# The gate products of a block-diagonal recurrence: four 64x64 tiles in place of a 128x128 weight with zero blocks

## The reference, cut to what matters

```python
xc = depthwise_conv(x, conv_w, conv_b, (LRU_CONV_WIDTH - 1, 0))      # 4 taps
xb = xc.reshape(xc.shape[:-1] + (LRU_BLOCKS, LRU_BLOCK))             # 8 blocks of 64
r = sigmoid(einsum("blhi,hij->blhj", xb, w_r).reshape(xc.shape) + b_r)
i = sigmoid(einsum("blhi,hij->blhj", xb, w_i).reshape(xc.shape) + b_i)
log_a = -LRU_C * r * softplus(-lam)
a = exp(log_a)
bx = sqrt(-expm1(2.0 * log_a)) * (i * xc)
# h[t] = a[t] * h[t-1] + bx[t], forward (d = 0) and backward (d = 1), context first
```

## Time and profile before

| | us |
|---|---|
| median of three runs | 1327.19 (1326.09 to 1328.32) |
| profiled execution, span from first to last instruction | 1326.2 |
| TensorE matmul busy | 1263.8 |
| VectorE busy | 730.9 |
| ScalarE busy | 533.8 |
| GpSimd busy | 8.2 |

### The profile page before, as it was taken

The page is one execution under the profiler, slowest core; times in us unless marked ns, Lnnn a source line. Parts: engine busy times, 40 slices in busy tenths (PEclk is TensorE's granted clock), DMA queues, the critical chain, the costliest instruction groups (busy, mean ns, idle before and its releaser), DMA issues.

```text
span 1326.2 us, 16470 instructions
## 1 busy us (share of the span) xinstructions
PE 1263.8 (95%) x6748; PEld 963.8 (73%) x6748; DVE 730.9 (55%) x1154; ACT 533.8 (40%) x837; POOL 8.2 (1%) x10
## 2 busy tenths in 40 slices
PE   3698999999999999999999999989999999999996
PEld 0254876777777777675777777758877998889995
DVE  2433435586665565553352333275799977755554
ACT  3322335542123334443342222244655464575452
POOL 1000000000000000000000000000000000000000
PEclk9898999999999999999999999989999999999998
DMA  9999335545543333332555544552332433325541
GB/s 369 352 338 335 138 136 228 233 196 206 208 179 125 121 147 127 127 127 98 193 197 210 210 175 186 206 191 95 128 127 93 154 136 127 128 96 191 179 171 64
DMA packets 56122, 233.69 MB, mean 176 GB/s; under 512 B 8048, under 2 KB 10224, under 8 KB 34160
## 3 DMA queue, kind: packets, MB, share of 16 engines
q1 hardware_dynamic: 56048, 232.65, 47.4%
HBM read 230.54 MB, written 2.10 MB: 175 GB/s over the span
## 4 chain that ended last, share of the span: by engine, by line
PE 84%; DMA 6%; DVE 5%; ACT 3%; issue 1%; SPq 0%; DVEq 0%; ACTq 0%
PE psum_block L576 21%; PE psum_block L578 20%; PE psum_block L577 20%; PE psum_ada L486 5%; DMA glu<-in_w_ada 3%; PE psum_scores L653 3%; PE psum_scores L631 2%; PE psum_scores L610 2%; DMA glu<-in_w_blocks 1%; DVE w_lo L1037 1%; DMA raw<-in_w_ada 1%; PE psum_scores L544 1%; PE psum_scores L546 1%; PE psum_scores L545 1%; PE psum_scores L644 1%; PE psum_block L544 1%
## 5 line engine op out<-in xcount | busy, mean ns | idle before, releaser
L576 PE MATMUL psum_block<-h_hi,w_hi 128*128 128x512 f32 (+1 forms) x1616 | 562.4, 348 | 0.7 <-ACT glu L1011 0.7
L577 PE MATMUL psum_block<-h_lo,w_hi 128*128 128x512 f32 (+1 forms) x1616 | 547.9, 339 | 0.0
L578 PE MATMUL psum_block<-h_hi,w_lo 128*128 128x512 f32 (+1 forms) x1616 | 547.7, 339 | 0.0
L1037 DVE TENSOR_TENSOR w_lo<-raw,w_hi 128x1024 fp32r<-128x1024 f32 x218 | 264.6, 1223 | 417.3 <-ACT w_hi L762 417.0
L762 ACT ACTIVATE w_hi<-raw 128x1024 fp32r<-128x1024 f32 x218 | 229.4, 1057 | 554.4 <-PE psum_block L578 521.4
L576 PEld LDWEIGHTS psum_block<-h_hi,w_hi 128*128 128x128 f32 x1616 | 306.4, 190 | 77.8 <-issue 38.3
L577 PEld LDWEIGHTS psum_block<-h_lo,w_hi 128*128 128x128 f32 x1616 | 306.6, 190 | 35.4 <-issue 3.8
L578 PEld LDWEIGHTS psum_block<-h_hi,w_lo 128*128 128x128 f32 x1616 | 306.5, 190 | 34.3
L1226 DVE SCALAR_TENSOR_TENSOR Y<-glu,small,Y 128x512 f32<-128x512 f32 (+1 forms) x240 | 130.4, 611 | 0.0
L486 PE MATMUL psum_ada<-raw,cstat 128*32 128x512 f32 x512 | 67.2, 616 | 5.5 <-DMA raw<-in_w_ada 5.5
L506 PE MATMUL psum_ada<-raw,cstat 128*32 128x512 f32 x200 | 33.7, 760 | 23.7 <-DMA raw<-in_w_ada 23.6
(11 more groups left out here) (158 smaller groups left out, 1042.2 us busy)
## 6 DMA issues: line engine op xcount, KB each, us to landing
raw<-in_w_blocks SPq DMA_DIRECT2D x106, 1024.0 KB, 4.8
raw<-in_w_ada SPq DMA_DIRECT2D x89, 1024.0 KB, 6.8
glu<-in_w_ada SPq DMA_DIRECT2D x7, 1024.0 KB, 9.5
Y<-in_xT SPq DMA_DIRECT2D x4, 1024.0 KB, 16.2
T<-in_xT SPq DMA_DIRECT2D x16, 256.0 KB, 7.1
glu<-in_w_blocks SPq DMA_DIRECT2D x3, 1024.0 KB, 10.4
raw<-in_w_blocks SPq DMA_DIRECT2D x6, 512.0 KB, 5.1
raw<-in_pw SPq DMA_DIRECT2D x2, 1024.0 KB, 6.1
```

The lines of the kernel that those rows point to most:

```text
L576: mm(ps[:, 0:n], hi, hh[:, k, t], start=(at == 0), stop=False)
L577: mm(ps[:, 0:n], hi, hl[:, k, t], start=False, stop=False)
L578: last = mm(ps[:, 0:n], lo, hh[:, k, t], start=False, stop=(at == DT - 1))
L1037: V.tensor_tensor(wl[:, u % 4, :], raw_of(item)[:, j * HALF:(j + 1) * HALF], wh[:, u % 4, :].bitcast(F32), ALU.subtract).then_inc(*C.up("l ...
```

## The change

The weights are stored without zeros (`bd` is half as wide), the memset and the wait for it go, and each of the four DMAs fills whole rows. For each direction d, four matmuls of 64 rows by 64 columns are issued in place of two of 128 by 128, one on each quarter of the array: half j of the channels gives r on its own partitions and i on the other half's partitions, both in PSUM bank 2d+j. ScalarE's tanh is done on 64 partitions at a time, eight instructions for four; those of i read from one half of the partitions and write to the other. The wait before the first exponential is written in another way and means the same.

```diff
-        bd = sb("bd", [P, 2, 2 * CT, P])
+        bd = sb("bd", [P, 2, 2 * CT, P // 2])
...
-                else:
-                    sp.wait_ge(*C.at("bd_zero"))
                 for g in range(2):
                     for j in range(2):
-                        sp.dma_start(bd[64 * j:64 * j + 64, g, :, 64 * j:64 * j + 64],
+                        sp.dma_start(bd[64 * j:64 * j + 64, g, :, :],
...
-            nc.gpsimd.memset(bd[:, :, :, :], 0.0).then_inc(*C.up("bd_zero"))
...
                 for d in range(2):
-                    for g in range(2):
-                        last = mm(psS[:, 2 * d + g, :], bd[:, g, d * CT + t, :], T[:, 4 * d, :], start=True, stop=True)
+                    for j in range(2):
+                        for g in range(2):
+                            r, o = 64 * j, 64 * (j ^ g)
+                            last = mm(psS[o:o + 64, 2 * d + j, :], bd[r:r + 64, g, d * CT + t, :], T[r:r + 64, 4 * d, :],
+                                      start=True, stop=True, tile_position=(r, o))
...
-                    fn(T[:, 4 * d + 1, :], psS[:, 2 * d, :], ACT.Tanh, scale=0.5, bias=hbr[:, c:c + 1]
-                       ).then_inc(*C.up("lru_tanh", l, t, d, "r"))
-                    fn(T[:, 4 * d + 2, :], psS[:, 2 * d + 1, :], ACT.Tanh, scale=0.5, bias=hbi[:, c:c + 1]
-                       ).then_inc(*C.up("lru_tanh", l, t, d))
+                    for j in range(2):
+                        r = slice(64 * j, 64 * j + 64)
+                        fn(T[r, 4 * d + 1, :], psS[r, 2 * d + j, :], ACT.Tanh, scale=0.5, bias=hbr[r, c:c + 1]
+                           ).then_inc(*C.up("lru_tanh", l, t, d, "r"))
+                    for j in range(2):
+                        r, o = slice(64 * j, 64 * j + 64), slice(64 - 64 * j, P - 64 * j)
+                        fn(T[r, 4 * d + 2, :], psS[o, 2 * d + j, :], ACT.Tanh, scale=0.5, bias=hbi[r, c:c + 1]
+                           ).then_inc(*C.up("lru_tanh", l, t, d))
```

More of the change, by code:

```diff
@@ L846, in lru_act @@
                     c = (l * 2 + d) * CT + t
-                    fn(T[:, 4 * d + 1, :], psS[:, 2 * d, :], ACT.Tanh, scale=0.5, bias=hbr[:, c:c + 1]
-                       ).then_inc(*C.up("lru_tanh", l, t, d, "r"))
-                    fn(T[:, 4 * d + 2, :], psS[:, 2 * d + 1, :], ACT.Tanh, scale=0.5, bias=hbi[:, c:c + 1]
-                       ).then_inc(*C.up("lru_tanh", l, t, d))
+                    for j in range(2):
[6 more added lines that the diff above has]
+                           ).then_inc(*C.up("lru_tanh", l, t, d))
                 for d in range(2):
                     c = (l * 2 + d) * CT + t
-                    act.wait_ge(*C.ago("lru_tanh", 2 - 2 * d + 1))
+                    act.wait_ge(*C.at("lru_tanh", l, t, d, "r"))
                     fn(T[:, 4 * d + 3, :], T[:, 4 * d + 1, :], ACT.Exp, scale=s4n[:, c:c + 1], bias=s4n[:, c:c + 1]
```

## The result

The changed kernel took 1337.49 us (median of 4 runs, 1335.71 to 1339.43) against 1327.74 us for the kernel before beside it (4 runs): a ratio of 1.0075, 95% interval 1.0061 to 1.0088. The forecast was 1324.7 and the range ended at 1331.0. The profiled span went from 1326.2 to 1337.5 us.

What follows compares the result with a forecast made beforehand. The prediction took TensorE, busy 95% of the span, as the bound, with a ring of dependences setting the time at points in layer 1; -3.4 (layer 0) +1.1 (layer 1) -0.2 (DMA) = -2.5 us gave 1324.7 us, range 1319.5 to 1331.

Steps and rivals of the forecast that it cites:

- TensorE's part: Gate products: quarter passes run four at once, 1.7 us per step; gains 1.6 us a step in layer 0, 1.4 in layer 1.
- rival B: Gate products: row halves don't run together, 3.4 us as before, with longer ScalarE work; +9.2 us, 1336.4; chance 0.11.
- ScalarE's part: Gate tanh: eight instead of four, starts still 0.57 us apart, adding 2.3 us to each step's ScalarE work.
- rival C: Gate tanh: crossing halves costs more, 0.69 us each, 3.2 us added per step; 1329.2 us; chance 0.08.
- Three steps pass clean: Layer 0: longer ScalarE work delays nothing TensorE needs in three steps, gaining 3 x 1.6 = 4.8 us.
- price of 0.7 us for a turn: Cycle of taps, products, tanh, VectorE work and scan: 2.3 longer tanh minus 1.6 earlier products, 0.7 us longer each turn.
- The wait for line 772: Layer 0 after step 3: TensorE's transposes wait 3 us for ScalarE's late line 772; layer 0 brings 3.4 us, not 6.4.
- Layer 1: Recurrence in layer 1: VectorE's late results delay TensorE, which leaves 1.1 us later than before.
- waits of about 3 us for the taps at steps 1 and 3: Layer 1: TensorE's waits for the convolution taps (line 1184) grow to about 3 us at these steps.
- The waits before blocks 9, 12, 13 and 18: Layer 1: new TensorE waits for line 1037 or 1127 expected before these blocks, as a sign of the forecast.
- Sum: Whole kernel: -3.4 for layer 0, +1.1 for layer 1, -0.2 for DMA, -2.5 us in all; 1324.7 us.
- DMA: Opening: weight DMAs without small pieces gain 0.2 us, between 0 and 1.5; those in layer 1 counted as nothing.

Runs made afterwards that it cites:

- second kernel: The changed kernel's quarter-tile products with ScalarE's tanh on all 128 partitions as in the kernel before (gates mixed up): 1320.23 us, ratio to before 0.9946.

## Why the prediction was wrong

- *TensorE's part* was right. Four at once, 1.9 us a step, 1.5 and 1.6 us gained at steps 0 and 1 of layer 0; rival B's mechanism is excluded, though its 1336.4 is near the measured time. A time that fits proves no cause.
- *ScalarE's part* took 0.57 a tanh; the upper bound, 0.69 in rival C, was near the measured 0.71. The row I took it from the earlier trace rows showed neighbours on the same partitions. The term was 2.3 us and is 3.37. Rival C priced this at 1329.2, 4.5 us above the forecast; the rest of the miss lies elsewhere.
- **The step that failed outright** is "Three steps pass clean" in layer 0. It counted TensorE's blocks and not VectorE's load between step 2 and step 3, where the taps before were done 0.2 us ahead of their use; and its price of 0.7 us for a turn let the products' 1.6 us pass on to the tanh in full, where at step 2 only 0.6 did, since ScalarE was not ready. From the first products to `lru_v` are 12.2 us there instead of 9.4. Forecast for that stretch -1.6, measured +2.5. With the tanh at 0.57 `lru_v` would have come 1.1 us earlier, and the wait would still have been some 2.8: it was there by either price. (The second kernel, whose full tanh take the 2.3 us less, waits 0.56 there.) The wait for line 772, which I did forecast at 3 us, came at 1.5 us, and later (296.95), since the lead had been lost by then. The +1.6 measured for that last stretch, so near the +1.4 forecast, is luck: with tiles and full tanh it takes 9.3 us (the second kernel), and to that come the wait's 1.5 and 1.8 us for the low clock at 285.7.
- *Layer 1*: the places were right, the sizes not. Forecast were waits of about 3 us for the taps at steps 1 and 3: 3.03 and 3.28, but they stand behind turns that are 1.8 us longer each instead of 0.7, so the sizes match by luck. The waits before blocks 9, 12, 13 and 18 are 2.76, 1.29, 1.46 and 1.79, where the working has 0.2 for block 12, 1.5 for block 18 and no size for the others. The clock, which the forecast left out, adds 1.4 us for each of two drops and something at the third, which was not taken apart. Forecast +1.1, measured +9.4.
- *Sum*: layer 0 missed by 4.4 us, layer 1 by 8.3, opening and middle together (+0.8 measured, -0.2 forecast) by 1.0: 13.7 of the 13.8 between the span's +11.3 and the forecast's -2.5.
- *DMA*: the 0.2 can't be told from the spread of the opening.

The Trainium skill (TensorEngine Tiling, Performance Considerations) warns that tiling speeds up TensorE but not the evacuation of PSUM. Here it is the whole loss: with the evacuation unchanged the tiles gain 7.2 us, with its instructions doubled they lose 9.8.

## What to carry to other kernels

A saving on the busiest engine is paid out only up to the next thing that engine waits for; follow every wait in the stretch, VectorE's queue between two steps too, and ask how early each input now stands before its use, and whether the engine that takes an earlier result is free to take it. When an operand's layout changes for one engine's sake, price the other engine's instructions by a row with the same change of partitions from one to the next, or take the worse bound. Look for a layout in which only the part that must cross is cut up, and put the cut part last in the chain.

## What the runs showed of the hardware

- ScalarE: neighbouring tanh of 512 columns out of PSUM start 0.57 to 0.585 us apart while the partitions read and written stay the same, at 128 and at 64 partitions; where the half read or the half written changes, 0.70 to 0.71.
- TensorE: fp32 matmuls on four 64x64 quarters run four at once, starts some 7 ns apart within a four and 0.43 us from four to four; row halves may write into one bank in turns without loss.
- TensorE's clock: 3.4 us or more at the lower level (1.2 of 2.4 GHz) at the end of 29 of 44 waits of 1.7 to 4 us; two drops in layer 1 cost 1.4 us each, one in layer 0 1.8.
